# A transformer kernel on one core: the moving operand of its dense matmuls read in another order and placed at other distances to the weights

## The reference, cut to what matters

```python
# first block, per layer
proj = h @ w_in[l]                       # 1024 -> 2594 columns, then three mixers
h = layer_norm(ALPHA * h + mixed @ w_out[l], ...)
ff = square(relu(h @ w_up[l])) @ w_down[l]        # 1024 -> 4096 -> 1024
h = layer_norm(ALPHA * h + ff, ...)
# second block, per layer
h = h + 0.5 * rms_norm(swiglu(rms_norm(h, g0), ffn_wi, ffn_wo), g1)   # 1024 -> 2 x 2816 -> 1024
y = attention(rms_norm(h, g2) @ wqkv) @ wo        # banded attention, another kind in each layer
h = h + rms_norm(y, g3)
h = h + 0.5 * rms_norm(swiglu(...), g5)           # a second gated feed-forward
h = h + rms_norm((p @ ple_proj) * sigmoid(rms_norm(h, g6) @ ple_gate), g7)
```

## Time and profile before

| | |
|---|---|
| median of the runs | 3431.65 us |
| the profiled execution, whole | 3430.66 us |
| its span, first to last instruction | 3428.8 us |
| mean granted TensorE clock | 0.988 of full speed |
| TensorE, matmuls | 3317.4 us busy, 97% of the span |
| TensorE, weight loads | 2633.9 us, 77% |
| VectorE / ScalarE / GpSimd | 54% / 36% / 10% |
| read from device memory | 296.14 MB, 87 GB/s over the span |

### The profile page before, as it was taken

The page is one execution under the profiler, slowest core; times in us unless marked ns, Lnnn a source line. Parts: engine busy times, 40 slices in busy tenths (PEclk is TensorE's granted clock), DMA queues, the critical chain, the costliest instruction groups (busy, mean ns, idle before and its releaser), DMA issues.

```text
span 3428.8 us, 42531 instructions
## 1 busy us (share of the span) xinstructions
PE 3317.4 (97%) x16570; PEld 2633.9 (77%) x16570; DVE 1836.8 (54%) x2932; ACT 1241.6 (36%) x1878; POOL 342.3 (10%) x244
## 2 busy tenths in 40 slices
PE   9999999999899999999999999999999989999997
PEld 6667888776688887888777778887788876688886
DVE  5776334567752446443566664435644357654436
ACT  3354222424442324332333342324432235532324
POOL 0310000212100020000233100000000012100001
PEclk9999999999999999999999999999999999999999
DMA  4102222311122222223322122232222321122232
GB/s 162 62 32 74 96 95 98 128 62 50 50 85 94 98 98 81 98 97 104 107 74 68 63 81 96 98 105 93 86 96 94 105 94 39 61 98 98 98 105 80
DMA packets 81431, 300.35 MB, mean 88 GB/s; under 512 B 9040, under 2 KB 9040, under 8 KB 80640
## 3 DMA queue, kind: packets, MB, share of 16 engines
q1 hardware_dynamic: 78624, 284.20, 24.8%
q0 software_dynamic: 1568, 11.98, 0.9%
q10 hardware_dynamic: 1088, 2.10, 0.2%
HBM read 296.14 MB, written 2.10 MB: 87 GB/s over the span
## 4 chain that ended last, share of the span: by engine, by line
PE 88%; DVE 6%; ACT 3%; issue 1%; POOL 1%; DMA 1%; ACTq 0%; DVEq 0%; POOLq 0%
PE bank L874 25%; PE bank L876 25%; PE bank L875 24%; PE bank L918 2%; PE bank L925 2%; PE bank L919 2%; DVE wl L2026 1%; PE bank L1411 1%; ACT sc L1710 1%; PE bank L1423 1%; PE bank L1175 1%; PE bank L1156 1%; ACT wh L1549 1%; PE bank L1466 1%; PE bank L1114 1%
## 5 line engine op out<-in xcount | busy, mean ns | idle before, releaser
L874 PE MATMUL bank<-x,wh 128*128 128x512 f32 x2632 | 1053.7, 400 | 14.8 <-DVE h L2470 5.7
L876 PE MATMUL bank<-x,wl 128*128 128x512 f32 x2632 | 1027.3, 390 | 0.0
L875 PE MATMUL bank<-x,wh 128*128 128x512 f32 x2632 | 1026.1, 390 | 0.0
L1549 ACT ACTIVATE wh<-raw 128x1024 fp32r<-128x1024 f32 x528 | 558.0, 1057 | 1171.6 <-PE bank L876 1083.6
L2026 DVE TENSOR_TENSOR wl<-raw,wh 128x1024 fp32r<-128x1024 f32 x528 | 677.7, 1284 | 567.4 <-ACT wh L1549 566.0
L874 PEld LDWEIGHTS bank<-x,wh 128*128 128x128 f32 x2632 | 494.9, 188 | 135.9 <-issue 29.4
L876 PEld LDWEIGHTS bank<-x,wl 128*128 128x128 f32 x2632 | 494.6, 188 | 105.4
L875 PEld LDWEIGHTS bank<-x,wh 128*128 128x128 f32 x2632 | 495.7, 188 | 98.4 <-issue 3.4
L874 PE MATMUL bank<-mid,wh 128*128 128x512 f32 x1216 | 474.9, 391 | 0.5 <-DVE wl L2026 0.5
L876 PE MATMUL bank<-mid,wl 128*128 128x512 f32 x1216 | 473.1, 389 | 0.0
L875 PE MATMUL bank<-mid,wh 128*128 128x512 f32 x1216 | 473.1, 389 | 0.0
(11 more groups left out here) (340 smaller groups left out, 3294.5 us busy)
## 6 DMA issues: line engine op xcount, KB each, us to landing
raw<-stream SPq DMA_DIRECT2D x528, 512.0 KB, 3.3
raw_apart<-stream SPq DMA_DIRECT2D x10, 512.0 KB, 3.6
sm<-small POOLq DMA_DIRECT2D x2, 2144.0 KB, 10.6
tb<-tab POOLq DMA_DIRECT2D x2, 1728.0 KB, 14.8
h<-x_t ACTq DMA_DIRECT2D x4, 512.0 KB, 6.8
out_t<-h SPq DMA_DIRECT2D x8, 256.0 KB, 2.1
tba<-tab_a POOLq DMA_DIRECT2D x1, 1152.0 KB, 8.5
pf<-p_t POOLq DMA_DIRECT2D x2, 512.0 KB, 3.9
```

What stands on the lines that cost most here:

```text
L874: pe.matmul(dst, hi, src[:, kc, 0, :], start=start, stop=False)
L875: pe.matmul(dst, hi, src[:, kc, 1, :], start=False, stop=False)
L876: return pe.matmul(dst, lo, src[:, kc, 0, :], start=False, stop=stop)
L1549: act.activation(high_of(n)[:, :], raw_of(n)[:, :], ACT.Copy).then_inc(hi_done, 1)
```

## The change

`x`, `px` and `mid` get a gap behind each chunk: 4 values (16 bytes) for `x` and `px`, 8 values (32 bytes) for `mid`. So chunk k begins 16k or 32k bytes later relative to its weights than before. And every dense matmul reads its 512 tokens, and writes its 512 outputs, in another order: 32 tokens from the first half of the chunk (tokens 0 to 31), 32 from the second half (256 to 287), then 32 to 63, 288 to 319 and so on: 16 pieces of 128 bytes. The products are the same.

```diff
+RUN = 32
+X_GAP, MID_GAP = 4, 8
...
+        def staggered(name, chunks, gap, offset=None):
+            t = at(name, [P, chunks, 2 * S + gap], F32R, offset)
+            return t[:, :, 0:2 * S].rearrange("p k (e s) -> p k e s", e=2)
...
-        x = at("x", [P, DC, 2, S], F32R)
+        x = staggered("x", DC, X_GAP)
+        place[0] += (x_at - place[0]) % 512
...
-        px = at("px", [P, 2, 2, S], F32R, offset=x_at + 6 * 2 * S * 4)
+        px = staggered("px", 2, X_GAP, x_at + 6 * (2 * S + X_GAP) * 4)
...
-        mid = at("mid", [P, FF2C, 2, S], F32R)
+        mid = staggered("mid", FF2C, MID_GAP)
...
-        apart_at = [mix_at + 6 * 2 * S * 4, y_at]
+        apart_at = [mix_at + 6 * (2 * S + MID_GAP) * 4, y_at]
...
+            def crossed(ap):
+                return ap.rearrange("p (b a c) -> p a b c", b=2, c=RUN)
...
             def piece(dst, u, col, src, kc, start, stop):
                 hi, lo = high_of(u)[:, col:col + P], low_of(u)[:, col:col + P]
-                pe.matmul(dst, hi, src[:, kc, 0, :], start=start, stop=False)
-                pe.matmul(dst, hi, src[:, kc, 1, :], start=False, stop=False)
-                return pe.matmul(dst, lo, src[:, kc, 0, :], start=False, stop=stop)
+                dst, x_hi_, x_lo_ = crossed(dst), crossed(src[:, kc, 0, :]), crossed(src[:, kc, 1, :])
+                pe.matmul(dst, hi, x_hi_, start=start, stop=False)
+                pe.matmul(dst, hi, x_lo_, start=False, stop=False)
+                return pe.matmul(dst, lo, x_hi_, start=False, stop=stop)
...
-                pe.matmul(dst, hi, x[:, kc, 0, :], start=kc == 0, stop=False)
-                pe.matmul(dst, lo, x[:, kc, 0, :], start=False, stop=False)
+                pe.matmul(crossed(dst), hi, crossed(x[:, kc, 0, :]), start=kc == 0, stop=False)
+                pe.matmul(crossed(dst), lo, crossed(x[:, kc, 0, :]), start=False, stop=False)
...
-                    mm = pe.matmul(dst, hi, x[:, kc, 1, :], start=False, stop=kc == 7)
+                    mm = pe.matmul(crossed(dst), hi, crossed(x[:, kc, 1, :]), start=False, stop=kc == 7)
```

## The result

The changed kernel takes 3532.51 us (median of 2 runs, 3532.01 to 3533.0), the kernel before 3431.65 us: ratio 1.0293, 95% interval 1.0268 to 1.0318. It is slower by 101 us. The profiled execution has a span of 3531.2 us, against 3428.8.

A forecast was written before the change was run, and what follows sets the result against it. TensorE's 12,720 dense matmuls, times the distance between their starts, were taken to bound the kernel. From 3430.66 us, 85 us less for order and gaps and nothing for the rest gave 3345 us; range 3300 to 3500 us (0.81).

The forecast's parts named there:

- What bounds the kernel: TensorE: 12,720 dense matmuls at 226.6 ns from start to start, 2882 us, 84% of the span.
- the splits: Weight splits on VectorE and ScalarE: ample cover for TensorE's faster pace, so no change in time.
- the DMAs: Weight traffic on the DMA engines: 92 GB/s becomes 95 in the steady stretch, no change in time.
- the shift of the buffers: Buffers behind `x` move by 512 bytes and keep their remainder: no change in time.
- the term for the order of reading and the gaps: Dense matmuls on TensorE: 220 ns each, 6.7 ns less, times 12,720 makes 85 us less.
- The bound of 216 ns: Loss-free dense matmul at full clock: at most 10.6 ns less each, 135 us over 12,720.
- Rival C: Dense reads and PSUM writes: each jump between pieces costs, 6.7 ns more per matmul, 3515 us; chance 0.15.
- Rival D: Dense matmuls: with changing distances steps never settle and stay at 231.4 ns, 61 us more, 3491 us; chance 0.11.
- Rival B: Dense matmuls: the loss isn't where the change looks, another pattern of the same cost, 3431 us; chance 0.32.
- the last matmul before attention: Without a load over it, it should be some 10 ns shorter than 389 ns; it was 388 and 397.
- The signs I named: Line 874 starts, `ao`/`bo` against `x` steps, ScalarE idle 85 us less; wrong if 226.6 ns stays or VectorE's split releases.
- A: Dense matmuls: the collisions shrink, 3345 us, its own range 3295 to 3362; chance 0.42.

The follow-up runs named there:

- e1: The changed kernel's order of reading and writing without the gaps, against the kernel before: 3539.79 us, ratio 1.0315.
- e3: e1 with the new order for the moving operand alone, outputs written contiguously: 3535.41 us.
- e2: The changed kernel's gaps with the old contiguous order, against the kernel before: 3483.32 us, ratio 1.0152.
- e18: Changed kernel without gaps, weights 128 bytes further, 128-byte pieces in swapped pairs (second, first, fourth, third, and so on): 3432.53 us.
- e9: The kernel before with everything between `x` and `mid`, weight buffers included, moved 64 bytes further: 3503.24 us.
- e11: The kernel before with everything between `x` and `mid`, weight buffers included, moved 128 bytes further: 3493.58 us.
- e15: The kernel before with everything between `x` and `mid`, weight buffers included, moved 192 bytes further: 3453.17 us.
- e5: e1 with pieces of 128 tokens (512 bytes) instead of 32: 3431.51 us, ratio 1.0002 against the kernel before.
- e6: e1 with pieces of 64 tokens (256 bytes) instead of 32: 3430.65 us.
- e4: e1 with the new order for the writes to PSUM alone, tokens read contiguously: 3431.65 us.
- e17: e2 (old order) with gaps of 256 bytes in `x` and none in `mid`: 3432.11 us.
- e10: The kernel before with everything between `x` and `mid`, weight buffers included, moved 32 bytes further: 3503.61 us.
- e8: The kernel before with 64 of 128 weight columns loaded and used in all but a tile's first and last chunk: 3455.05 us.
- e16: The kernel before with 32 of 128 weight columns loaded and used in all but a tile's first and last chunk: 3467.19 us.
- e14: e1 with the weights 64 bytes further: 3537.55 us.
- e13: e1 with the weights 128 bytes further: 3540.81 us.

## Why the prediction was wrong

**What bounds the kernel** held: TensorE's steps are the time, nothing else moved, and the splits, the DMAs and the shift of the buffers cost nothing.

**The step that failed** is the term for the order of reading and the gaps: 6.7 ns less per matmul (220 ns), 85 us less. The runs gave 9.7 ns more (236.3 ns), 101 us more. The order alone gave 10.0 ns more (e1), all of it in reading the tokens (e3), and the gaps alone 5.3 (e2). The term was argued in three steps, and none of them held.

- From the earlier trace rows I took the shortest step, about 0.22 us (the starts printed there show 0.23 and 0.24), as a sign that the loss can shrink. The mean of the same seven steps is 231.4 ns, more than the settled 226.6: the row spoke for a rise.
- "Within one piece the reads are as contiguous as before" looked at the length of a piece. What counts is how the addresses modulo 256 bytes follow each other: 16 pieces of 128 bytes cost 10.0 ns in one sequence (e1) and nothing in another (e18).
- "Where addresses decide which reads collide, order and distance can move it" allows both directions, and the kernel before stood at a special point, all distances 0 modulo 256 bytes, that the gaps could only leave. No row before showed whether that point is good or bad; e9 to e11 and e15 show that it is the best of five.

The bound of 216 ns was never reached: no run of this case has dense matmuls that settle below 226.6 ns at the full clock.

**Rival C** (each jump costs; 3515 us) had the right sign and nearly the right size, 85 us against 101, by luck: its mechanism isn't there. Jumps are free (e5, e6, e18), and so are the PSUM writes (e4). The rule of the Trainium skill ("SBUF — State Buffer", section "Door 1: The DMA port swizzle") that a non-contiguous PSUM access slows matmuls, doesn't show at runs of 128 bytes: e4 has 226.7 ns.

**Rival D** (the settled state is lost; 3491 us, 231.4 ns) is what the gaps alone do: e2 has 3483.3 us and 232.0 ns. The rows behind a break gave nearly its price; that the cause is the same isn't shown. And it is not the varying that costs: e17 varies and settles, e9 and e10 don't vary and cost more.

**Rival B** rested on the last matmul before attention, which is no shorter with no load over it. e8 and e16, which find no gain from smaller loads, don't refute that. What I drew from it, that order and distance would be without effect, didn't follow. The rule of the Trainium skill that the prediction names ("SBUF — State Buffer", "Who interferes with whom": an independent port for weight loads, TensorE waits on nobody) would give the distance no price. The runs differ: 32 to 128 bytes cost 6.7 ns a matmul in e9 to e11.

**The signs I named**: 660 ns between starts of line 874 for A, 700 or more for C, 694 for D. It is 709 (236.3 x 3) and uneven. The unevenness is no mark of the gaps: e1, without gaps, has the same 397 to 403 ns. The products from `bo` do differ from those of `x` where the gaps stand alone (e2), as I said they should if the gaps cost. VectorE's split as a releaser could be no sign, since it was one before. I said ScalarE's idle time would fall by 85 us; it grew by 82.

**Still open.** Why a matmul of full rate loses 13.3 ns at all, and whether a weight load costs a fixed part of it (theory F), wasn't settled. Nor is it shown what within SBUF has the period of 256 bytes. Why pieces of 64 bytes cost 13.3 ns more and of 128 bytes 10.0, and why distance 192 costs a third of what 32 to 128 cost, isn't explained either. No version beat the kernel before; e5, e6, e17 and e18 equal it.

## What to carry to other kernels

Where TensorE is the bound and reads 4-byte values at full rate, compare its step from start to start with columns / clock, and try first to have the moving operand and its weights start at the same remainder of 256 bytes; that was worth up to 2% here. Reordering the moving operand was free in pieces of 256 and 512 bytes; pieces of 128 bytes were free only where the addresses modulo 256 ran on. And before a disorder is forecast to help, ask whether the present state is a special point: one uniform shift of the weight buffers told it here in a single run.

## What the runs showed of the hardware that I had not expected

- The loss per matmul is settled by addresses modulo 256 bytes: 226.6 ns at distance 0 and at changing multiples of 256 (e17), 233.3 ns at 32 and 64, 228.9 ns at 192. Within one run, e9, the two values stand side by side for the same tokens.
- A 16-fold interrupted write to PSUM and a stream with backward jumps cost nothing against the kernel before (e4, e18).
- The crossed read in pieces of 128 bytes costs 10.0 ns at distances 0, 64 and 128 alike (e1, e14, e13).
- The new order and the gaps cost nothing at the half clock: 426.7 ns before and after.
- Narrower weight loads made the steps longer, 230.0 and 231.7 ns (e8, e16), not shorter.
